# Moving the low halves of two weight tiles from VectorE's substitution to GpSimd in a bidirectional DeltaNet and RG-LRU layer

## The reference, cut to what matters

```
proj = h @ w_in
qkv  = silu(short_conv(proj[q, k, v]))                 # 4 taps, per channel
kk   = (k * beta) k^T * decay                          # per chunk and direction
tmat = strict_lower(kk) + I
u, w = triangular_solve(tmat, [v * beta, k * beta * exp(g)])
scan over the chunks: v_new = u - w S;  o = q_dec S + attn v_new;  S = gl S + k_dec^T v_new
o_dn = rmsnorm(o_fwd + o_bwd) * silu(z)
o_rg = (h_fwd + h_bwd) * silu(gate)                    # h = a h + b, a linear recurrence per channel
y    = x + gate_mod * rmsnorm([o_dn, o_rg] @ w_out)
```

## Time and profile before

| what | value |
|---|---|
| median of three executions | 1292.92 us (1292.5 to 1295.2) |
| the profiled execution's own time | 1293.07 us |
| its span in the trace | 1291.4 us |
| PE matmul, busy | 1220.1 us, 94% |
| DVE, busy | 991.5 us, 77% |
| ACT, busy | 732.1 us, 57% |
| POOL, busy | 135.7 us, 11% |
| mean granted clock of PE | 0.987 of full speed |

### The profile page before, as it was taken

How to read it: one execution, slowest core, us unless ns; L and a number is a source line. 1 busy time by engine, 2 the same in 40 slices (tenths; PEclk the granted TensorE clock), 3 DMA queues, 4 the chain that set the end, 5 groups by cost and what they waited for, 6 DMA issues and landing times.

```text
span 1291.4 us, 24187 instructions
## 1 busy us (share of the span) xinstructions
PE 1220.1 (94%) x8648; PEld 1091.5 (85%) x8648; DVE 991.5 (77%) x2038; ACT 732.1 (57%) x1728; POOL 135.7 (11%) x137
## 2 busy tenths in 40 slices
PE   6899999999999999999999999999996797999997
PEld 3599889998999899899989998998985656788886
DVE  4775899999899989899998999898999749422221
ACT  3643667648665865676486658656775738111110
POOL 3000001001010100010010101000100000422120
PEclk9899999999999999999999999999998999999999
DMA  7413021112111211211121112112111094534340
GB/s 309 144 33 95 19 59 46 52 52 75 29 52 38 85 35 34 74 50 52 52 75 30 46 41 87 35 34 70 53 52 52 17 370 129 159 102 118 94 126 32
DMA packets 95287, 100.29 MB, mean 78 GB/s; under 512 B 4389, under 2 KB 81446, under 8 KB 94154
## 3 DMA queue, kind: packets, MB, share of 16 engines
q1 hardware_dynamic: 92234, 88.38, 21.9%
q0 software_dynamic: 2944, 10.49, 2.1%
HBM read 83.55 MB, written 15.30 MB: 77 GB/s over the span
## 4 chain that ended last, share of the span: by engine, by line
PE 50%; DVE 32%; issue 9%; ACT 6%; DVEq 1%; SPq 0%; DMA 0%; POOL 0%; ACTq 0%; POOLq 0%
PE bank L1087 15%; DVE arena L1811 6%; DVE arena L1809 6%; PE bank L755 5%; PE bank L756 5%; PE bank L757 5%; DVE arena L1650 4%; PE bank L970 3%; DVE w_lo L1565 3%; DVE arena L1776 2%; PE bank L1062 2%; PE bank L1073 2%; PE bank L1031 2%; PE bank L1024 2%; PE bank L1047 2%
## 5 line engine op out<-in xcount | busy, mean ns | idle before, releaser
L755 PE MATMUL bank<-hT_hi,w_hi 128*128 128x384 f32 (+1 forms) x1182 | 435.6, 369 | 18.8 <-DVE w_lo L1565 14.1
L757 PE MATMUL bank<-hT_hi,w_lo 128*128 128x384 f32 (+1 forms) x1182 | 401.6, 340 | 0.0
L756 PE MATMUL bank<-hT_lo,w_hi 128*128 128x384 f32 (+1 forms) x1182 | 401.6, 340 | 0.0
L755 PEld LDWEIGHTS bank<-hT_hi,w_hi 128*128 128x128 f32 x1182 | 224.8, 190 | 29.9 <-DVE w_lo L1565 16.3
L756 PEld LDWEIGHTS bank<-hT_lo,w_hi 128*128 128x128 f32 x1182 | 225.1, 190 | 6.0 <-issue 0.3
L757 PEld LDWEIGHTS bank<-hT_hi,w_lo 128*128 128x128 f32 x1182 | 223.9, 189 | 0.0
L1650 DVE SCALAR_TENSOR_TENSOR arena<-arena 128x1154 f32<-128x1154 f32 x96 | 140.9, 1468 | 5.8 <-DVE arena L1650 3.3
L1407 ACT ACTIVATE arena<-bank,arena 128x128 f32<-128x128 f32 x272 | 78.0, 369 | 105.6 <-PE bank L1047 105.5
L1087 PE MATMUL bank<-wo_hi,ot_hi 128*128 128x512 f32 x288 | 113.3, 393 | 8.4 <-DVE wo_lo L1962 6.8
L1087 PE MATMUL bank<-wo_lo,ot_hi 128*128 128x512 f32 x288 | 112.7, 391 | 0.0
L1087 PE MATMUL bank<-wo_hi,ot_lo 128*128 128x512 f32 x288 | 112.6, 391 | 0.0
(11 more groups left out here) (238 smaller groups left out, 2164.4 us busy)
## 6 DMA issues: line engine op xcount, KB each, us to landing
w_raw<-w_in SPq DMA_DIRECT2D x51, 512.0 KB, 4.0
arena<-scr_G SPq DMA_DIRECT2D x16, 576.0 KB, 4.9
arena<-x_sample SPq DMA_DIRECT2D x16, 512.0 KB, 7.5
arena<-ada_w SPq DMA_DIRECT2D x8, 1024.0 KB, 17.0
wo<-w_out SPq DMA_DIRECT2D x4, 2048.0 KB, 15.8
ot<-scr_o SPq DMA_DIRECT2D x7, 1024.0 KB, 6.6
scr_o<-arena POOLq DMA_DIRECT2D x8, 576.0 KB, 3.7
scr_o<-arena POOLq DMA_DIRECT2D x8, 512.0 KB, 2.9
```

The lines of the kernel that those rows point to most:

```text
L755: pe.matmul(out, w_hi[:, slot, k], hT_hi[:, k, cols], start=first, stop=False)
L756: pe.matmul(out, w_hi[:, slot, k], hT_lo[:, k, cols], start=False, stop=False)
L757: return pe.matmul(out, w_lo[:, slot, k], hT_hi[:, k, cols], start=False, stop=last)
```

## The change

The low halves of the z and gate tiles (j = 4 and 5) are made by POOL, right behind its memset of `Zt` and ahead of `store_oz`, and no longer by DVE ahead of steps 7 and 22. They get a semaphore of their own, `w_lo_made_g`, on which PE waits for these two tiles. The waits of the other four `low_w` compare with the same numbers as before; they are only written by `w_hi_made.at`, since `w_lo_made` now counts four per head.

```diff
-        w_lo_made = Count(sem("w_lo_made"), 9, 6)
+        w_lo_made = Count(sem("w_lo_made"), 7, 4)
+        w_lo_made_g = Count(sem("w_lo_made_g"), 2, 2)
...
+            def low_w(slot, b, n):
+                gp.wait_ge(w_hi_made.sem, w_hi_made.at(b, n))
+                gp.tensor_tensor(w_lo[:, slot], w_raw[:, slot], w_hi[:, slot].bitcast(F32), ALU.subtract)\
+                  .then_inc(w_lo_made_g.sem, 1)
...
                 gp.memset(Zt, 0.0).then_inc(Zt_cleared.sem, 1)
+                low_w(0, b, 5)
+                low_w(1, b, 6)
...
-                    if u % 24 == 0:
+                    if u % 24 == 0 and j < 4:
                         pe.wait_ge(w_lo_made.sem, w_lo_made.at(b, j + 1))
+                    elif u % 24 == 0:
+                        pe.wait_ge(w_lo_made_g.sem, w_lo_made_g.at(b, j - 3))
...
                 for k in range(1, BLK - 1):
-                    if k == 7:
-                        low_w(0, w_lo_made.at(b, 5))
                     if k == 14 and not first:
                         gate_o(b)
-                    if k == 22:
-                        low_w(1, w_lo_made.at(b, 6))
```

More of the change, by code:

```diff
@@ L1753, in phase_a @@
                     conv(2, xf, b + 1, 2)
-                    low_w(0, w_lo_made.at(b, 3))
+                    low_w(0, w_hi_made.at(b, 3))
                     conv(2, xf, b + 1, 3)
@@ L1787, in phase_a @@
                 if first:
-                    low_w(1, w_lo_made.at(b, 4))
+                    low_w(1, w_hi_made.at(b, 4))
                 for t in range(1, 4):
@@ L1848, in joins @@
                 if not last:
-                    low_w(0, w_lo_made.at(b, 1))
+                    low_w(0, w_hi_made.at(b, 1))
                 rg_piece("ix", 0, b)
@@ L1881, in background @@
                         if step == 3:
-                            low_w(1, w_lo_made.at(b, 2))
+                            low_w(1, w_hi_made.at(b, 2))
                         for j, t in TAPS[step]:
```

## The result

The changed kernel takes 1307.47 us (median of 8 runs, 1304.97 to 1308.93), the kernel before beside it 1292.95 us (8 runs, 1292.5 to 1301.15). The ratio is 1.0101, with 95% between 1.0084 and 1.0118: slower, by 14.5 us where 8.8 were forecast (1301.7). The profiled run of the changed kernel took 1306.2 us and its span 1304.6, 13.2 us more than the span before. Its granted clock was 0.985, before 0.987.

The account below looks back on a forecast made before the run. It took PE's join to hang on DVE's substitution and ACT's square, within half a microsecond. Seven phases at 1.32 us (9.2) and -0.4 in the last gave +8.8: 1301.7 us, range 1296 to 1308.

Parts of the forecast that it names:

- Exclusion: In DVE's substitution, each POOL subtraction stops DVE's steps and costs 2.02 us instead of 1.22; the forecast, chance 0.68.
- rival B: POOL finds no gaps between substitution steps and makes the low halves late; +4 to +5 us, 1297 us, chance 0.12.
- Rival A: POOL reads during the substitution without stopping DVE, which has 2.44 us less; 1290.5 or 1287.8 us, chance 0.12.
- Rival C: Taking turns at its upper bound, plus growing ACT and DVE waits in the scan; 1306 to 1312 us, chance 0.08.
- the two overlaps of the earlier trace: POOL select and DVE step overlapping by 0.20 and 0.16 us, taken off POOL's 2.38 us to give 2.02.
- DVE's and PE's delay per phase: At the substitution's end, DVE's last transpose and PE's q32 each come 1.60 us later per phase.
- The wait for ACT's square: DVE's 0.50 us wait at its next step behind the transposes vanishes, as the square is done by then.
- join32 and the head: PE's join32 comes 1.32 us later, carried through seven phases: 9.2 us; a head takes 119.8 us instead of 118.5.
- PE has no slack from there on: From join32 on PE idles only 1.8 us per head, so the 1.32 us delay is carried through in full.
- The last phase: The last phase_a saves 1.22 us for z beside a transpose and loses 0.80 for the gate: -0.4 us.
- The range: 1296 to 1308 us for the changed kernel; chance of being slower by over 0.2% 0.86.
- exclusion at its full length: Each POOL subtraction costs DVE 2.38 us with no overlap; +16.6 us in all, 1309.5 us.

Follow-up runs that it names:

- p1: Kernel before, DVE keeping its low halves, with two more POOL memsets per phase at the change's times; 1293.35 us, ratio 0.9994.
- e5: Kernel before with only z's low half on POOL, released just ahead of gate_o, which moves from step 14 to 9; 1291.11 us, ratio 0.9964.
- p3: Kernel before, DVE keeping its low halves, with two POOL multiplications by 0 of one SBUF input per phase; 1305.99 us, ratio 1.0086.
- e4: The changed kernel with two units of PE's projections moved from behind q32 to ahead of it; 1300.36 us, ratio 1.0057 to the kernel before.
- e1: Kernel before with only z's low half moved to POOL, the gate's staying on DVE; 1295.95 us, ratio 1.0027.
- e2: Kernel before with only the gate's low half moved to POOL, z's staying on DVE; 1298.30 us, ratio 1.0051.
- p2: Kernel before, DVE keeping its low halves, with two POOL subtractions of two SBUF inputs per phase; 1325.91 us, ratio 1.0243.
- a2_change_again: The changed kernel itself, unaltered, run and profiled a second time; 1308.72 us, ratio 1.0097 to the kernel before.
- e7: Kernel before with both low halves on POOL in seven later phases, z's beside gate_o at step 11, gate's beside the closing transposes; 1294.56 us, ratio 1.0001.

## Why the prediction was right and where it fell short

**Exclusion, the two engines taking turns: right, in kind and in size.** The prediction took 2.02 us for what a POOL subtraction costs DVE, and it is 2.08. Two steps of 2.35 and 2.48 us stand where 2.3 was named. POOL did not starve (rival B): with 2.41 us it got in between two short steps. Rival A, free reading, is out by the same rows. Rival C's 1306 to 1312 us takes in the measured time, but not for its reasons: a held step costs 2.08 us and not 2.38, and the heads without a drop of the clock have the forecast's length. The held step lost 0.3 us less than POOL's instruction lasted (2.08 for 2.41); the two overlaps of the earlier trace rows are 0.36. Not everything on either engine took part: POOL's memsets of 2.02 us held nothing (p1, longest step 0.41 us), gate_o, which reads PSUM and one SBUF input, was not held by a subtraction of 2.38 us (e5, 1.79 us as without it), and POOL's multiplication of one SBUF input, 2.78 us long, held the step for 0.73 us only (p3).

**DVE's and PE's delay per phase: right.** The transposes were to end 1.60 us later, and end 1.57 later behind the memset (43.32 for 41.75). Two holds of 2.08 us alone would make it 1.72; the last transpose happened to take 1.89 us for 2.03. q32 was to come 1.60 later and comes 1.56 later. The wait for ACT's square at DVE's next step was to vanish and has.

**join32 and the head: the head right by luck, the path to it a little off.** join32 was to come 1.32 us later and comes 1.55 later (47.16 for 45.61). The prediction took PEld's 0.28 us of idling ahead of join32 for slack, since the row names DVE. After the change DVE is in time, and PEld idles there all the same:

```profile
791.20 0.10 PEld L944 LDWEIGHTS bank<-arena 32*32 32x32 f32 x1 [0.25 <-issue]
```

So all but 0.03 us of it was no wait for DVE. The head is nevertheless only 1.34 us longer: 0.2 us come back in the scan, at the group of four matmuls shown above, which no part of the sum foresaw.

**The clock: the step that failed.** The prediction has "PE has no slack from there on" and a sum in which work behind q32 keeps its duration. It stretched PE's wait ahead of q32 from 0.4 to 2.0 us and gave that wait no price but its length. The hint stood in the earlier trace rows: q32 itself took 1.12 us behind the 5.04 us wait, for 0.81 elsewhere. What the runs showed instead: behind a wait of 2.0 us PE's clock falls to 0.50 for some 3.4 us in some phases, and such a head is 1.7 us longer still (121.59 - 119.91 = 1.68; for the first phase 2.99 - 1.34 = 1.65). e4 is the test: the same DVE costs, a wait of 1.1 us, no drop ahead of the last phase, and 1300.36 us, 1.3 from the forecast. e1 and e2 agree (waits to 1.35 us, no drop in a middle head, and the two excesses sum to the forecast's size), and p2 from the other side (3.3 us and more, a drop in each). By that price the profiled run, with two drops, has 3.3 us from the clock. The median lies 14.5 us over before: seven heads at 1.34 and -1.3 for the last phase are 8.1. How the other 6.4 divide is an estimate, as the timed runs have no trace: four drops, or three and a start that comes 1.5 to 2 us later, as it does in both profiles of the change. The second profile has three drops in the first seven phases and one in the last. The mean granted clock, which is on record for every run, points the same way: it was 0.980 to 0.983 in the seven other runs of the change, 0.985 in the profiled one with its two drops, and 0.984 or 0.985 in all of e4.

**The last phase: right in kind, off in size.** z's low half beside the transpose was taken as free and is: the transpose at 992.75 stands beside POOL's subtraction of 992.78 and takes 2.02 us, for 1.98 before. No trace of before showed that the transpose's single SBUF input would spare it; the price of nothing was the author's estimate. Beside the select of the earlier trace rows DVE's tensor_scalar of one SBUF input took 1.77 us, where the shortest at line 1648 takes 0.81. The gate's cost 2.24 us (a step of 2.63 for 0.39) and not 2.02. The first closing transpose also takes 2.25 us there for 2.04. So the substitution ends 0.06 us later instead of 0.4 earlier; but from the last memset to the end it is 1.3 us shorter. The prediction said that PE's wait ahead of the last q32 would only lengthen; it fell from 5.04 to 1.68 us, since PE now waits 4.04 us for ACT earlier in that phase (line 876, until 1009.14). In this profile the clock behind the last q32 is 1.00, before it was 0.73. In the second profile the wait is 2.76 us, the clock 0.67, and the gain 0.6 us, so that it is not a sure one.

**The range** held the median by half a microsecond, and that was luck. It reached up to 1308 us for the sake of exclusion at its full length (whose 1309.5 it did not even take in); the missing cost was of another kind. The four runs of `a2_change_again` have their median at 1308.72, outside it.

## What to carry to other kernels

Moving a subtraction from VectorE to GpSimd took nothing off VectorE here, where it ran beside steps with two SBUF inputs: it cost them 2.08 of its 2.41 us, where VectorE itself needs 1.22. The same operation held up neither a transpose by more than 0.1 us (e7) nor the step that reads PSUM (e5, 1.79 us with and without it), so try such a place (what reached past the PSUM step held the next one for 0.44 us), and ask first whether the engine that is relieved sets the end at all: the chain gave the substitution 12%, and taking both operations away altogether was worth 0.24%. When TensorE's wait in a dense stretch is stretched toward 2 us, price the clock behind it as well (1.65 us for each drop here; drops stood behind waits of 1.7 us and more, none behind waits up to 1.35), and try filling the wait with TensorE's own later work.

## What the runs showed of the hardware that was not expected

- Behind a wait of 2.0 to 2.2 us in a stretch where PE is otherwise busy, the granted clock fell to 0.50, for some 3.4 us, in two of the first seven phases of one profile and three of seven in another of the same kernel; a head with such a drop was 1.5 to 1.9 us longer than those without. Waits up to 1.35 us brought none in the first seven phases of any profile, waits of 1.7 to 1.8 us (p3) two, and waits of 3.3 us (p2) one in each. The slower timed runs of the kernel before (1294.6 to 1299.1 us) have a mean granted clock of 0.978 to 0.984, its faster ones (up to 1293.4 us) 0.982 to 0.987; none of the slower ones was profiled, so where they lose it stays open.
- A POOL tensor_scalar of one 128x1024 input takes 2.78 us, longer than the two-input subtraction with 2.41, and yet holds a DVE step for 0.7 to 0.9 us, not for 2.08.
- A POOL subtraction whose inputs are one and the same tensor takes 1.9 to 2.0 us, with two tensors 2.4.
- POOL got in between DVE steps that depend on each other and stand 0.03 us apart, within the time of one step; beside independent subtractions of DVE the first instruction at line 686 lasted 7.56 us, 5.2 more than the second.
